# Sample-group attention run inside the prompt attention of a two-layer decoder step

## The reference, cut to what matters

```
D_MODEL = 1024; SEQ = 1024; DEPTH = 2; DEC_BATCH = 8; DEC_SEQ = 1
PAST_LEN = 2048; PAGE_SIZE = 128; N_HEADS = 16; N_KV_HEADS = 4; HEAD_DIM = 64; D_FF = 2816

# stick: z = q k^T * scale, past = key_pos < pos
log_keep = where(past, log_sigmoid(-z), 0)
log_between = cumsum(log_keep, reverse=True) - log_keep
w = where(past, exp(log_sigmoid(z) + log_between), 0);  o = w @ v

# fox: decay from a running sum of log_f
p = softmax(where(key_pos <= pos, z + cum[pos] - cum[key], -inf));  o = p @ v

# each layer
x = x + mixer(rms_norm(x)) @ w_o;  x = x + conv_ffn(rms_norm(x))
```

## Time and profile before

| | us |
|---|---|
| median of 3 runs | 3334.87 (3334.8 to 3341.08) |
| profiled execution | 3341.93 |
| its span | 3340.3 |
| PE busy | 2987.0 (89% of the span) |
| DVE busy | 1584.9 (47%) |
| ACT busy | 850.3 (25%) |
| POOL busy | 877.4 (26%) |
| granted PE clock, mean | 0.958 |

### The profile page before, as it was taken

The page is one execution under the profiler, slowest core; times in us unless marked ns, Lnnn a source line. Parts: engine busy times, 40 slices in busy tenths (PEclk is TensorE's granted clock), DMA queues, the critical chain, the costliest instruction groups (busy, mean ns, idle before and its releaser), DMA issues. The chain is left out here.

```text
span 3340.3 us, 52291 instructions
## 1 busy us (share of the span) xinstructions
PE 2987.0 (89%) x18964; PEld 2775.9 (83%) x18964; DVE 1584.9 (47%) x2199; ACT 850.3 (25%) x1120; POOL 877.4 (26%) x675
## 2 busy tenths in 40 slices
PE   6978788867999999999999897986699999999994
PEld 6967677634999999999989797974299999999994
DVE  5167777432443433434451888754144433334345
ACT  3035455321211111111220444431032111111121
POOL 2124344323222232223221331031322222322220
PEclk8989899989999999999999998997999999999997
DMA  2100000535111111111111111052511111111111
GB/s 105 42 11 1 1 1 1 174 106 157 42 51 38 50 51 50 38 38 50 52 34 49 37 26 36 20 162 81 174 64 39 51 38 39 53 59 38 38 39 51
DMA packets 138706, 182.58 MB, mean 55 GB/s; under 512 B 15591, under 2 KB 120529, under 8 KB 138502
## 3 DMA queue, kind: packets, MB, share of 16 engines
q1 hardware_dynamic: 122078, 145.91, 13.5%
q0 software_dynamic: 16480, 34.70, 3.8%
HBM read 171.74 MB, written 8.99 MB: 54 GB/s over the span
## 5 line engine op out<-in xcount | busy, mean ns | idle before, releaser
L337 PE MATMUL psum<-x_hi,w_hi 128*128 128x344 f32 x2688 | 579.4, 324 | 4.2 <-issue 2.7
L337 PE MATMUL psum<-x_lo,w_hi 128*128 128x344 f32 x2688 | 572.8, 321 | 0.0
L337 PE MATMUL psum<-x_hi,w_lo 128*128 128x344 f32 x2688 | 570.3, 321 | 0.0
L337 PEld LDWEIGHTS psum<-x_hi,w_hi 128*128 128x128 f32 x2688 | 453.0, 189 | 7.0 <-issue 4.2
L337 PEld LDWEIGHTS psum<-x_lo,w_hi 128*128 128x128 f32 x2688 | 456.9, 190 | 0.0
L337 PEld LDWEIGHTS psum<-x_hi,w_lo 128*128 128x128 f32 x2688 | 450.9, 189 | 0.0
L870 DVE TENSOR_TENSOR xT<-psum,xT 128x1032 f32<-128x1032 f32 x176 | 216.9, 1232 | 288.0 <-PE psum L337 288.0
L716 POOL TENSOR_TENSOR w_lo<-raw,w_hi 128x2048 fp32r<-128x2048 f32 x44 | 203.3, 4621 | 419.5 <-ACT w_hi L712 419.5
L857 POOL TENSOR_TENSOR act_lo<-gate,act_hi 128x1032 fp32r<-128x1032 f32 x44 | 106.2, 2413 | 719.3 <-ACT act_hi L828 719.3
L337 PE MATMUL psum<-act_hi,down_hi 128*128 128x344 f32 x1056 | 225.8, 322 | 12.8 <-issue 12.8
L878 DVE TENSOR_TENSOR a_pad<-psum,rstd 128x1032 f32<-128x1032 f32 x44 | 54.2, 1232 | 384.2 <-PE psum L337 384.2
(11 more groups left out here) (253 smaller groups left out, 4778.4 us busy)
## 6 DMA issues: line engine op xcount, KB each, us to landing
raw<-in_ffn_w_a_dram SPq DMA_DIRECT2D x22, 1024.0 KB, 5.1
raw<-in_ffn_w_b_dram SPq DMA_DIRECT2D x22, 1024.0 KB, 5.1
raw<-in_ffn_w_down_dram SPq DMA_DIRECT2D x22, 1024.0 KB, 4.9
dc_page<-in_cache_k_dram SPq DMA_DIRECT2D x128, 128.0 KB, 2.4
dc_page<-in_cache_k_dram POOLq DMA_DIRECT2D x128, 128.0 KB, 2.6
dc_page<-in_cache_v_dram POOLq DMA_DIRECT2D x128, 128.0 KB, 2.8
dc_page<-in_cache_v_dram SPq DMA_DIRECT2D x128, 128.0 KB, 2.6
raw<-in_w_qkv_dram SPq DMA_DIRECT2D x10, 1024.0 KB, 4.9
```

What stands on the lines that cost most here:

```text
L337: last = nc.tensor.matmul(out[:, c, 0:NG], w[:, k, cols], r(k)[:, c * NG:(c + 1) * NG], start=(k == 0 and part == 0), stop=(k == kt - 1 an ...
```

## The change

stick_prompt, fox_prompt and decode are replaced by one function attention(l), which holds both groups in one stage. Its parts:

- Steps. The two hardware loops of 8 heads are one written-out list of 128 steps N. Within a head the query blocks come in the order 0, 7, 1, 6, 2, 5, 3, 4, so that steps of 1 to 4 blocks and steps of 8 to 5 blocks alternate; scores of the first kind lie in one PSUM bank, of the second in two others.
- PE. In a step N: transposes of N, transposes of cached key pages, values of N-1, scores of the key pages of step N-1, prompt scores of N+3, sums over value pages. The cached work is cut in 64 units of two pages: keys at steps 2 to 59, values at steps 72 to 125. A key unit has 4 transposes and 4 f32 products with the transposed page as weights (128 x 128) and 8 query columns moving; a value unit has 4 f32 products with the page as weights and 8 columns of attention weights moving. The products with high and low parts of cached keys, the zeroing products and the turns of outputs are gone.
- DVE and ACT. The high parts of keys and queries are made by ACT, the low parts by DVE (which waits for ACT); the scale is applied when q leaves the projection (a multiply by a scalar joined to the one that was there). ACT copies the transposed key pages, DVE copies each sequence's scores.
- The soft-plus, suffix sums and softmax of the samples are placed at steps between 61 and 75. The sums over later pages are added up on DVE from the summands themselves, and PE multiplies them by ones.
- Fox values are computed as in the stick layer (64 output rows per head, transposed weights moving), and POOL scales the probabilities by the reciprocal before they are transposed; the output turns and their copies are gone.
- DMA. All pages are loaded from SP, into 6 key slots and 8 value slots of two pages; in layer 1 SP also loads the cached log-forget rows. ACT loads the decay rows.

```diff
-        nc.vector.tensor_tensor(thirds(target(n)), acc[p % 2][:, :, 0:NG], thirds(rstd[:, :]), ALU.mult)
+        nc.vector.scalar_tensor_tensor(out=thirds(target(n)), in0=acc[p % 2][:, :, 0:NG], scalar=1.0 if n < 4 else SCALE,
+                                       in1=thirds(rstd[:, :]), op0=ALU.mult, op1=ALU.mult).then_inc(s_free, 1)
...
+        ORDER = (0, 7, 1, 6, 2, 5, 3, 4)
+        K_SLOTS, V_SLOTS = 6, 8
+            K_FIRST, K_OVER = 2, 58
+            V_FIRST, V_OVER = PER_TURN + 8, 54
+            k_step = [K_FIRST + u * K_OVER // UNITS for u in range(UNITS)]
+            v_step = [V_FIRST + u * V_OVER // UNITS for u in range(UNITS)]
...
+                    for u in range(UNITS):          # SP
+                        if u >= K_SLOTS:
+                            sp.wait_ge(s_t, of_unit[u - K_SLOTS] + 1)
+                        for j in range(2):
+                            pid = sp.value_load(pages[0:1, 2 * u + j:2 * u + j + 1], min_val=0, max_val=POOL - 1)
+                            sp.dma_start(kpage[u % K_SLOTS][:, j, :],
+                                         cache_k[l, bass.ds(pid, 1)].rearrange("a t g d -> t (a g d)")).then_inc(...)
...
+                    for N in range(STEPS + 1):      # PE
+                        if N < STEPS:
+                            turn(N)
+                            for u in units_at(k_step, N):
+                                turn_keys(u)
+                        if N >= 1:
+                            values(N - 1)
+                            for u in units_at(k_step, N - 1):
+                                score_keys(u)
+                        if N + 3 < STEPS:
+                            scores(N + 3)
+                        for u in units_at(v_step, N):
+                            sum_values(u)
...
+                        for j in range(2):          # score_keys(u)
+                            for hf in range(HALVES):
+                                c = b % 2 * NPAGE * NH + (n + j) * NH + hf * HH
+                                last = nc.tensor.matmul(dec[:, c:c + HH], kt[u % 2][:, (2 * j + hf) * P:(2 * j + hf + 1) * P],
+                                                        qd[:, hf, b, :], start=True, stop=True)
...
+                    def prepare(h):                 # DVE
+                        low_queries(h)              # waits for ACT's high part
+                        if h % HG == 1 and h // HG >= 1 and h // HG + 1 < NKV:
+                            low_keys(h // HG + 1)
...
+                    for N in range(STEPS + 1):      # DVE
+                        if fox and N + 1 < STEPS:
+                            invert(N + 1)
+                        if N + 2 < STEPS:
+                            read_scores(N + 2)
+                        if N < STEPS:
+                            copy_turned(N)
+                        if heads_prepared_at(N) is not None:
+                            prepare(heads_prepared_at(N))
+                        if N >= 1 and (N - 1) % ST >= ST - 2:
+                            store_o(N - 1)
...
+                        if N == CUM - 1:
+                            sums_of_later_pages()
+                        if 0 <= N - CUM < 4:
+                            add_sums(N - CUM)
...
+                    for N in range(STEPS):          # ACT
+                        copy_turned(N)
+                        for u in units_at(k_step, N):
+                            copy_keys(u)
+                        if N + ahead < STEPS:
+                            mid(N + ahead)          # stick: two sigmoids, ahead = 3; fox: exp, ahead = 2
+                        if heads_prepared_at(N) is not None:
+                            prepare(heads_prepared_at(N))
+                        if not fox and N == SCORED + 1:
+                            soft_plus()
+                        if N == V_FIRST - 1:
+                            weigh()
```

More of the change, by code:

```diff
@@ L1598, in trunk_program, with attention, tile @@
[L1598 to L1604 removed]
+        def attention(l):
             fox = l == 1
[L1609 to L1610 removed]
+            NP1 = NPAGE + 1 if fox else NPAGE
             off = [W]
[L1613 removed]
+            def tile(name, shape, dt=F32, end=W + WBYTES):
@@ L1616, in tile @@
                     n *= x
-                t = at(f"dc_{name}{l}", shape, off[0], dt)
+                t = at(f"{name}_{l}", shape, off[0], dt)
                 off[0] += n + (-n % 32)
-                assert off[0] <= LOGF
+                assert off[0] <= end, name
                 return t
-            page = [tile(f"page{j}", [P, 4, KVD]) for j in range(BUFS)]
-            turned_hi = [tile(f"turned_hi{j}", [P, HALVES, 4 * P], F32R) for j in range(2)]
-            score = tile("score", [P, NB, PG, NH])
@@ L1659, in page_loop @@
-            def page_loop(engine, body):
-                with engine.Fori(0, NB // 2) as bb:
-                    for u in range(2):
-                        body(bb, u)
-            def page_semaphores(name):
-                even = [sem(f"{name}_buffer{j}") for j in (0, 2)]
-                return [even[0], s_pool_page[0], even[1], s_pool_page[1]]
-            def pages_loaded(stage, bb, n):
-                before = 64 * (2 * l + stage) * (NB * NPAGE // (4 * BUFS)) if n % 2 else 0
-                return before + 64 * (TURN // BUFS * bb + n // BUFS + 1)
@@ L1682, in decode @@
[L1682 to L1693 removed]
+            k_hi = tile("k_hi", [P, 2, SEQ], F32R)
@@ new lines, in attention @@
+            k_lo = tile("k_lo", [P, 2, SEQ], F32R)
+            queries = [tile(f"queries{s}", [P, SEQ], F32R) for s in range(2)]
+            ident_q, mask_q = tile("ident_q", [P, P], F32R), tile("mask_q", [P, P], F32R)
+            rows = [tile(f"rows{j}", [P, SEQ]) for j in range(ROWS)]
+            score = tile("score", [P, NB, NP1, NH])
+            qd = tile("qd", [P, HALVES, NB, HH])
+            pages = tile("pages", [1, NB * NPAGE], I32)
+            stat = tile("stat", [P, 4, 4])
+            vnew = tile("vnew", [P, HALVES, NB])
@@ new lines, in attention @@
+            off[0] = TAIL
+            if fox:
+                ncum = [tile(f"ncum{j}", [P, SEQ], end=W) for j in range(2)]
+                logf = tile("logf", [P, NB, NPAGE, NH], end=W)
+                small = tile("small", [P, 4, NB * NH], end=W)
+            else:
+                keep = [tile(f"keep{j}", [P, SEQ + 1], end=W) for j in range(PB)]
+                zero = tile("zero", [P, SEQ], end=W)
+            wt = [at(f"wt{j}_{l}", [P, SEQ], R2 + 2 * TILE + j * SEQ * 4) for j in range(2)]
@@ new lines, in attention @@
+            summand = logf if fox else part
+            z_ps = [psum[:, 2, :], flat(0, 2)]
+            t_ps = [psum[:, 3, :], psum[:, 4, :]]
+            o_ps = [psum[:, 5, :], psum[:, 6, :]]
+            dec = psum[:, 7, :]
+            s_once, s_khi, s_k, s_qhi, s_q = (sem(f"at_{n}_{l}") for n in ("once", "keys_hi", "keys", "queries_hi", "queries"))
+            s_z, s_mid, s_read, s_w = (sem(f"at_{n}_{l}") for n in ("scores", "mid", "scores_read", "weights"))
+            s_t, s_ta, s_td = (sem(f"at_{n}_{l}") for n in ("turned", "turned_act", "turned_dve"))
@@ new lines, in attention, with units_at @@
+            CUM = SCORED + 2 if fox else PER_TURN + 2
+            SUMS = NPAGE - 1 if fox else NPAGE + 1
+            WEIGHED = 1 if fox else 4
+            def units_at(table, N):
+                return [u for u in range(UNITS) if table[u] == N]
+            groups, of_step, of_unit = [], {}, {}
+            for N in range(STEPS):
+                for j0 in range(0, ORDER[N % ST] + 1, 4):
+                    of_step.setdefault(N, []).append(len(groups))
+                    groups.append((j0, "act" if sum(1 for g in groups if g[0] is not None) % 2 == 0 else "dve"))
+                for u in units_at(k_step, N):
+                    of_unit[u] = len(groups)
+                    groups.append((None, "act"))
@@ new lines, in copies, with wait_copied, head_of, block_of @@
+            def copies(g):
+                return sum(1 for x in groups[:g + 1] if x[1] == groups[g][1])
+            def wait_copied(engine, g):
+                engine.wait_ge(s_ta if groups[g][1] == "act" else s_td, copies(g))
+            def head_of(N):
+                return N // ST
+            def block_of(N):
+                return ORDER[N % ST]
+            def keys_of(N):
+                return (block_of(N) + 1) * P
+            def buffer_of(N):
+                return z_ps[block_of(N) // 4]
```

1213 lines of the change are left out of this document (414 added, 799 removed).

## The result

The changed kernel is slower: 3447.57 us (3440.92 to 3451.51) against 3337.97 on the same chip, a ratio of 1.0326, interval [1.0303, 1.0349]. The forecast was 3180, range 3085 to 3275, with 0.06 on slower. Size and sign are both wrong.

What follows compares the result with a forecast made beforehand. A two-step loop through PE, ACT and DVE bounds stick, PE bounds fox: 3341.93 - 73 (layer 0) - 88 (layer 1) + 5 (SP) = 3186, less 7 for the median, predicted as 3180 us, range 3085 to 3275.

Steps and rivals of the forecast that it cites:

- 33.3 a head, PE's own 29.8: Layer 0 key stretch: a stick head takes 33.3 us by the loop with half the page scores; PE's work alone 29.8.
- 30 for the value stretch: Layer 0 value stretch: PE 26.5 us a head, loop 29.5, and 30 taken because the stalls are uneven.
- the loop: Stick layer: scores, sigmoids, scan, DVE copy, values, next scores close over two steps; 27.3 us a head, 29.5 with queries.
- half clock only at the start: Layer 0's attention: 5 us added for half clock at the start.
- The queries: Stick loop: the low part on DVE stands ahead of the 8-block scan and waits for ACT's high part; 2.2 us a head.
- Small products: PE's cached work: each product with 128 weight columns and 8 moving costs 0.107 us, between bounds of 0.026 and 0.112.
- The fox layer: Layer 1's attention: PE bounds it, 29.8 us a key head and 26.5 a value head; 482 us against 570.1.
- POOL's pass: Fox layer: POOL's pass with a scalar, not in the trace, taken as 2.0 us for 8 blocks.
- (a): Rival: PE bounds both layers, since sigmoids and scans overlap PE's work better; 465 us a layer, 3079 in all; chance 0.16.
- (b): Rival: page copies on ACT and score copies on DVE lengthen the loop in both layers; 3249 us; chance 0.25.
- (c): Rival: slower than before, the loop closes over every step, 50 us a stick head; 3430 us; chance 0.04.
- (d): Rival: pages come too late to hide the samples, needing 6 us and more a unit instead of 3.5; chance 0.03.

Runs made afterwards that it cites:

- e2: Changed kernel, but in layer 0 DVE copies the transposed weights of step N before it scans step N+2; 3303.49 us.
- e3: Changed kernel, but in layer 0 PE's prompt scores of step N+3 stand ahead of the values of N-1 and the key pages' scores; 3313.58 us.
- e9: Changed kernel with e1 and, in layer 0, the key pages' transposes behind the values of N-1 instead of ahead of them; 3339.86 us.
- e1: Changed kernel, but in layer 0 DVE makes the low part of the next queries three steps later, behind the 8-block scan; 3403.08 us.
- e12: Changed kernel plus 26 unread products on PE ahead of the waiting values in six value-stretch heads of layer 0; 3425.77 us.
- f1_timed: Changed kernel, both layers queries late, key transposes behind values; layer 0 also copy before scan, scores before values; 3193.07 us, ratio 0.9562 to the kernel before.

## Why the prediction was wrong

**The step that failed** is "33.3 a head, PE's own 29.8" for the stick key stretch, with 30 for the value stretch. It failed in two ways.

First, the wait stands earlier than I put it. I let the loop run through the values, with key transposes as work that PE puts in between. In the queue they stand ahead of the values and need the bank whose copy is behind the scan, so they are a waiter and not a cover; the values and page scores queue behind them. In the turn above the wait ends at 326.51 and the next large step's scores start at 335.56: all of PE's work of those 9 us stands in the loop, where I had counted only the values and half of the page scores. Idle time is 11.8 us a head, not 3.5. Shown by the waits; e2 and e3 take most of it away by cutting the loop, and e9, which moves only the waiter, takes a part (8.7).

Second, I priced a wait at its own length. In the changed kernel's layer 0 waits of 2.8 to 3.6 us are followed by some 6 to 20 us at clock 0.50 (10 behind the one of 2.84 us above, 20 behind one of 2.97 us that ends at 772.1). That is some 13 of the 24 us missing in a key head and some 7 of the 8 in a value head. Shown for the value stretch by e1 (-8.5 us of busy time with the same products) and by e12; for the key stretch it is worked out from the busy times and the clock of the windows. In the sum: 7.25 key heads x 24.4 = 177 and 6.75 value heads x 8 = 54 are 231; the last heads, the middle and the start took 79 against 99, which leaves the 211 between 754 and 543. I had put in half clock only at the start, 5 us, a term that no row shows.

**The queries** (+2.2 a head): mechanism right, ACT's copy 1.05 against 1.02 taken, idle 2.8. Its price was wrong for the second reason; with it out of the way value heads are at 29.4 to 31.1.

**Small products** at 0.107: right. In the turn above 8 of them start at 319.96 and the next kind at 320.87, 0.91 in all against the 0.86 of the forecast, and the bound of 0.026 was the wrong one. (1024 of them at 25 ns would have saved 84 us, not 82; nothing hangs on it.) The key transposes were too cheap: in e2, 4 start at 292.58 and the next kind at 293.11, 0.13 each and 0.15 in the turn before, against 0.109; 1 us a key head, of the 3 or so by which PE's own 29.8 was too low. The rest of the 3 isn't taken apart.

**The fox layer**, 482 forecast, 538.4 measured. Value heads 27.5 and 28.4 against 26.5: PE full at 1.00, as named. Key heads 37.5 in the mean against 29.8: PE busy 33.8, idle 3.7, clock down to 0.88 in places, with the same waiter. "PE above 95% in the key stretch" was false (34.0 of 37.2). With queries late and key transposes behind the values it took 502.0 to 503.1, so some 36 of the 56 us go with those two edits, which were not told apart; the remaining 20 are PE's own 31.4 a key head and the middle stretch, not taken apart either.

**POOL's pass** was unknown: 2.85 for 8 blocks, where I took 2.0.

```profile
L1670 POOL TENSOR_SCALAR rows<-rows,stat 128x1024 f32<-128x1024 f32 x16 | 45.5, 2847 | 53.2 <-DVE stat L1419 53.2
```

It cost little that shows: in the whole run PE waits for it 5 times, 7.7 us in all, and is full in fox's value heads with it.

**The rivals.** (a) PE bounds both: no, PE does it only in layer 1's value stretch. (b) the copies of pages and of page scores come into the loop: half right, since the page's work did come into the loop, but as the waiter, and in the whole run no row has PE waiting for a page's copy; I gave it 36 a head and it took 57.7. (c) slower: its sign was right, and its 3430 lies closest to the 3447.57, but by luck: its mechanism was that every step closes the loop. There are 27 waits in 48 steps, so the loop has two steps, as I had it, and not one. Its threshold was useful: 38 us a head for layer 0, and the heads passed it. (d) pages: no row has a DMA of pages as releaser of PE in these stretches.

Open: the middle of layer 0, where two heads take 36 and 42 us in f1_timed. PE there waits once for ACT's copy and once for the samples' suffix sums on DVE:

```profile
482.83 0.45 PE L1253 MATMUL psum<-ident,rows 128*128 128x128 f32 x1 [8.16 <-ACT wt L1617]
...
503.81 2.05 PE L1312 MATMUL psum<-part,tri_incl 128*128 128x512 f32 x2 [9.87 <-DVE later L1456]
```

Open is also whether ACT's copy, put ahead of its sigmoids, would give more; it is the larger wait left in e2 (30.8 us). Neither was tried. The changed kernel and the reordered one were each timed against the kernel before, not against each other; with 7.4% between them that matters little.

## What to carry to other kernels

When work is put between the links of a chain as cover, look in the instruction order whether its first instruction needs anything of the same chain, a buffer too: then it is a waiter and hides nothing. Price a repeated PE wait of about 3 us as itself plus the slow stretch that can follow in the granted clock, here some 13 us beside 11.8 of idle time in a key head, 8.5 beside 2.2 in a value head. Read that clock behind each wait: it doesn't always fall. In e2 a wait of 3.24 us ended at 281.86 and the clock stayed at 1.00:

```profile
282.00:285.00 3.00, 3.00 (x26) 2.66 (x27) 2.94 (x4) 0.60 (x1) 0.00 (x0) 1.00 0.15 47
```

And before giving up a reordering that lost, look for the one edge (here a copy behind a scan) that closes the loop: the same work ran 7.4% faster with four positions changed.

## What the runs showed of the hardware

PE at 1.00 fell to 0.50 in idle times of 2.84 and 3.64 us and stayed there with PE full for some 10 and at least 6 us; behind one of 3.24 us in e2 it stayed at 1.00. Unread products of 3.1 us in six such gaps kept it at 1.00 in four of the five heads behind them and made the kernel 22 us shorter. POOL's pass with one scalar for each partition took 2.85 us for 128 x 1024, its product of two tensors 2.0: the pass with fewer inputs is the slower. f32 products with 8 moving columns cost as much as those with 64, some 0.11 each (8 in 0.91, from 319.96 to 320.87), when 128 columns of weights are loaded for each.
